# The expert weights of a mixture-of-experts encoder layer: four-chunk transfers for experts 4 to 27, and two chunks of expert 3 read ahead of the down projection of expert 2

## What is computed

```
logits = ht.astype(jnp.float32) @ router_w.astype(jnp.float32) + router_b.astype(jnp.float32)
top_vals, top_idx = lax.top_k(logits, TOP_K)
weights = jax.nn.softmax(top_vals, axis=-1)
...
for e in range(N_EXPERTS):
    gu = ht @ w_gate_up[e] + b_gate_up[e]
    gate, up = gu[:, :D_FF], gu[:, D_FF:]
    gate = jnp.minimum(gate, SWIGLU_LIMIT)
    up = jnp.clip(up, -SWIGLU_LIMIT, SWIGLU_LIMIT)
    act = gate * jax.nn.sigmoid(SWIGLU_ALPHA * gate) * (up + 1.0)
    out = out + combine[:, e:e + 1] * (act @ w_down[e] + b_down[e])
```

## Time and profile before

| | |
|---|---|
| median of three runs | 1233.26 us |
| the profiled execution, its own time | 1233.55 us |
| its span in the trace | 1231.6 us |
| TensorE busy | 97% of the span |
| DMA engines busy from 320 us to 1200 us | 100% |
| VectorE, ScalarE busy | 36%, 22% |
| expert loads of 4 MiB, of 2 MiB | 53, 64 |

### The profile page before, as it was taken

The page is one execution under the profiler, slowest core; times in us unless marked ns, Lnnn a source line. Parts: engine busy times, 40 slices in busy tenths (PEclk is TensorE's granted clock), DMA queues, the critical chain, the costliest instruction groups (busy, mean ns, idle before and its releaser), DMA issues.

```text
span 1231.6 us, 13787 instructions
## 1 busy us (share of the span) xinstructions
PE 1189.2 (97%) x5866; PEld 641.0 (52%) x5866; DVE 437.9 (36%) x745; ACT 269.4 (22%) x440; POOL 0.2 (0%) x4
## 2 busy tenths in 40 slices
PE   9999999999999999999999999998999999889987
PEld 7899968888533443354444334433533444334332
DVE  7777878755422221212322222211222213112112
ACT  5876546344210000000100000000100101000002
POOL 0000000000000000000000000000000000000000
PEclk9999999999999999989999999999999999999999
DMA  9454425698999999999999999999999999999996
GB/s 317 154 163 146 150 90 172 217 399 340 363 424 428 428 427 427 429 436 429 426 435 429 428 434 432 428 433 434 425 432 432 429 428 433 431 425 426 428 425 253
DMA packets 59660, 455.26 MB, mean 370 GB/s; under 512 B 6122, under 2 KB 22923, under 8 KB 39118
## 3 DMA queue, kind: packets, MB, share of 16 engines
q1 hardware_dynamic: 58022, 454.06, 89.6%
q10 hardware_dynamic: 1576, 0.30, 0.1%
HBM read 453.29 MB, written 1.05 MB: 369 GB/s over the span
## 4 chain that ended last, share of the span: by engine, by line
PE 79%; DMA 16%; DVE 3%; issue 1%; ACT 1%; DVEq 0%; ACTq 0%
PE bank L1245 27%; PE bank L1263 15%; DMA ring<-in_w_gate_up 13%; PE total L935 6%; PE bank L935 5%; PE bank L993 4%; PE total L923 4%; PE bank L923 4%; DMA ring<-in_w_down 3%; PE bank L1231 2%; PE bank L1012 1%; PE total L1277 1%; PE bank L1252 1%; PE total L1245 1%; DVE qk_area L2187 1%
## 5 line engine op out<-in xcount | busy, mean ns | idle before, releaser
L1245 PE MATMUL bank<-ring,hy_area 128*64 128x512 f32 x1984 | 439.7, 596 | 14.6 <-DMA ring<-in_w_gate_up 14.6
L1245 PEld LDWEIGHTS bank<-ring,hy_area 128*64 128x64 f32 x1984 | 145.4, 137 | 289.7 <-issue 259.8
L1263 PE MATMUL bank<-ring,xn_area 128*64 128x512 f32 x992 | 223.3, 602 | 2.4 <-DMA ring<-in_w_down 2.4
L1263 PEld LDWEIGHTS bank<-ring,xn_area 128*64 128x64 f32 x992 | 74.0, 138 | 135.0 <-issue 124.9
L2184 DVE TENSOR_SCALAR qk_area<-bank 128x512 f32<-128x512 f32 x31 | 21.4, 692 | 328.2 <-PE bank L1245 328.2
L1728 ACT ACTIVATE qk_area<-qk_area 128x512 f32<-128x512 f32 x32 | 20.2, 630 | 428.3 <-DVE qk_area L2184 428.3
L2199 DVE SCALAR_TENSOR_TENSOR xn_area_r<-bank,tmp_area,xn_area_r 128x512 fp32r<-128x512 f32 x31 | 23.3, 751 | 206.1 <-ACT xn_area_r L1746 206.1
L1883 DVE TENSOR_TENSOR front_r<-ring,slot_r 128x1024 fp32r<-128x1024 f32 x60 | 73.0, 1222 | 19.5 <-ACT slot_r L1539 19.4
L1746 ACT ACTIVATE xn_area_r<-bank,tmp_area 128x512 fp32r<-128x512 f32 x31 | 21.3, 687 | 239.5 <-PE bank L1263 225.7
L1539 ACT CAST slot_r<-ring 128x1024 fp32r<-128x1024 f32 x60 | 62.8, 1050 | 43.6 <-PE bank L935 23.2
L1012 PE MATMUL bank<-tmp_area_r 128*128 128x512 f32 x124 | 40.5, 448 | 12.7 <-issue 8.6
(11 more groups left out here) (403 smaller groups left out, 1282.4 us busy)
## 6 DMA issues: line engine op xcount, KB each, us to landing
ring<-in_w_gate_up SPq DMA_DIRECT2D x33, 4096.0 KB, 29.1
ring<-in_w_gate_up SPq DMA_DIRECT2D x50, 2048.0 KB, 24.7
ring<-in_w_down SPq DMA_DIRECT2D x20, 4096.0 KB, 31.9
ring<-in_w_in SPq DMA_DIRECT2D x31, 1024.0 KB, 5.6
ring<-in_w_down SPq DMA_DIRECT2D x14, 2048.0 KB, 18.5
ring<-in_w_gate_up SPq DMA_DIRECT2D x22, 1024.0 KB, 9.3
ring<-in_w_down SPq DMA_DIRECT2D x19, 1024.0 KB, 9.8
ring<-in_w_branch_gla SPq DMA_DIRECT2D x4, 1024.0 KB, 5.1
```

The source lines that it names most:

```text
L1245: last = pe.matmul(to[bk][half * CAP:(half + 1) * CAP, :], xeT[:, j, q, :], where(j, c), start=False, stop=(j == GU_CH - 1), skip_group_ch ...
L1263: last = pe.matmul(banks[to][half * CAP:(half + 1) * CAP, :], half_of(turned, f), where(j, c * D + half * 512), start=(f == 0), stop=(f == ...
```

## The change

Three tables of numbers are changed. `AHEAD` gets an entry for expert 2: gate-up chunks 0 and 1 of expert 3 stand ahead of the down chunks of expert 2, in the loads and in the use. The one range `WIDE` becomes two: down transfers of four chunks (eight rows) for experts 4 to 29 (`BY_EIGHTS`), and gate-up transfers of four chunks (four rows) for the groups 1 to 6, experts 4 to 27 (`BY_FOURS`). Before, both held for experts 8 to 27.

```diff
-AHEAD = {0: (4, 6), 1: (0, 2)}
+AHEAD = {0: (4, 6), 1: (0, 2), 2: (0, 2)}
...
-WIDE = (8, E - QUAD)
-
-
-def wide(e):
-
-    return WIDE[0] <= e < WIDE[1]
+BY_EIGHTS = (4, E - 2)
+BY_FOURS = (1, E // QUAD - 1)
+
+
+def by_eights(e):
+
+    return BY_EIGHTS[0] <= e < BY_EIGHTS[1]
...
 def by_fours(g):
 
-    return WIDE[0] <= QUAD * g < WIDE[1]
+    return BY_FOURS[0] <= g < BY_FOURS[1]
...
-        if wide(e) and j % 4 == 0 and slot_of(n) + 4 <= SLOTS:
+        if (by_fours(e // QUAD) if j < GU_CH else by_eights(e)) and j % 4 == 0 and slot_of(n) + 4 <= SLOTS:
             width = 4
...
-                             rows_of(e, j, width, 4 if by_fours(e // QUAD) else 2, 8 if wide(e) else 4)).then_inc(moe_loaded[s], 16)
+                             rows_of(e, j, width, 4 if by_fours(e // QUAD) else 2, 8 if by_eights(e) else 4)).then_inc(moe_loaded[s], 16)
...
-                if wide(e):
-                    pe.wait_ge(actT_rest, e - WIDE[0] + 1)
+                if by_eights(e):
+                    pe.wait_ge(actT_rest, e - BY_EIGHTS[0] + 1)
...
-                elif wide(e):
+                elif by_eights(e):
                     copy_by_eights(e + 1)
```

More of the change, by code:

```diff
@@ L2179, in take_weights, with swiglu @@
                 nc.vector.tensor_copy(cslot[:, columns], source).then_inc(cslot_ready, 1)
-            def swiglu(used, count, made=banks[0:2], by_eights=False):
+            def swiglu(used, count, made=banks[0:2], reorder=False):
                 dve.wait_ge(chunks_used, used)
@@ L2189, in swiglu @@
                 dve.wait_ge(sigm_ready, count)
-                if by_eights:
+                if reorder:
                     u, g = (m.rearrange("p (m b c) -> p m b c", b=2, c=4) for m in (up, sig))
@@ L2228, in _ @@
                 g, q = e // QUAD, e % QUAD
-                swiglu(PLACE[e, GU_CH - 1] + 1, e + 1, gu_banks(e), wide(e))
+                swiglu(PLACE[e, GU_CH - 1] + 1, e + 1, gu_banks(e), by_eights(e))
                 if q == QUAD - 1 and g < GROUPS - 1:
```

## The result

The changed kernel takes **1236.59 us** (median of 8 runs, 1236.38 to 1238.80), the kernel before 1233.14 us beside it (8 runs). The ratio is 1.0034, with a 95% interval of 1.0024 to 1.0043: slower by 3.4 us by the medians, 3.0 to 5.3 by the interval. The profiled execution took 1236.38 us, its span is 1234.6 us.

What follows compares the result with a forecast made beforehand. The stream of expert weights through saturated DMA engines was taken as the bound. Terms of -0.7, 0, 3.3 and 0.9 us summed to +3.5 on the profiled 1233.55, giving a median of 1236.7 us, range 1232.5 to 1239.0.

Steps and rivals of the forecast that it cites:

- What bounds the kernel: Saturated DMA engines streaming expert weights set the end; PE work is free unless a load's lead falls under 2.6 us.
- Term A: Wider transfers: 52 chunks of experts 4 to 7, 28 and 29 go from two to four per transfer; -0.7 us.
- Term B: Two chunks of expert 3 ahead of expert 2's down: expert 4's first load has 4.2 us lead; cost 0.
- Term C: Expert 3's longer stall from the gather by four delays expert 5's first load; the stream stands for 3.3 us.
- F: Issue time of expert 5's first load: 428.0 with a short clock drop, 426.8 with clock kept, 430.0 with long drop.
- rival 1: The clock is kept in expert 3, the stream stands 2.1 us there; sum +2.3, 1235.6 us; 20% chance.
- short drop: Main forecast: lowered clock at expert 3's gather, as in expert 11, stall of 14.9 us; 1236.7 us, 37%.
- The signs: DMA share under 1 at 427 to 431 us, gather weight loads twice as long, granted clock under 1.00 there.
- rival 2: Expert 3's gather has the long clock drop, as in expert 7; sum +5.5, 1238.8 us; 22% chance.
- long drop: Lowered clock at expert 3's gather as in expert 7, stall of 16.9 us; the stream stands for 5.3 us.
- Term D: Expert 6's first load awaits down chunk 9 of expert 4; lead 1.7 us, the stream stands another 0.9 us.
- Rival 3: The queue never runs dry, with expert 3's stall at most 11.6 us; only the wider transfers' gain remains: 1232.6 us; 15%.

Runs made afterwards that it cites:

- e5: The kernel before with 2.0 us more TensorE work (repeated transposes) in expert 3; 1233.20 us, ratio 0.9997.
- d4: The kernel before with one wait moved, so the second pair of expert 5 is issued four chunks later, planned lead 0.5 us; 1236.85 us.
- d5: The kernel before with one wait moved, so the second pair of expert 5 is issued five chunks later, planned lead -2.5 us; 1240.12 us.
- e1: The changed kernel with gate-up of experts 4 to 7 back at two rows and two chunks per transfer, gather by two; 1233.16 us.
- e9: The changed kernel with gather by two for experts 4 to 7 and four-chunk gate-up transfers (two 16 KiB pieces) only from expert 6's chunk 4; 1232.87 us.
- e7: The changed kernel without the two chunks of expert 3 ahead of expert 2's down chunks; 1236.92 us.
- e2: The changed kernel with gather by four kept, but gate-up of experts 4 to 7 loaded two chunks at a time; 1235.02 us.
- e8: The changed kernel with the first gate-up transfers of experts 5 and 6 split into pairs; 1235.40 us.
- e4: The changed kernel with expert 3's four transposes done four times over, 2.0 us more planned on TensorE; 1237.77 us.
- e3: The changed kernel with only the first transfer of expert 5 (chunks 0 to 3) split into two pairs; 1236.65 us.
- e6: The changed kernel with gather by two; four-chunk gate-up transfers for experts 4 to 7 bring two pairs of rows each; 1235.29 us.

## Why the prediction was right, and where it was not

**What bounds the kernel** held: e5 adds PE time without effect, d4 and d5 take away lead alone and cost all of it.

**Term A** (-0.7 us) is too small to be seen in the medians: e1 with 24 of the 52 chunks and e9 with more are 0.2 and 0.1 us faster, within their intervals. In the changed kernel's trace it stands as 0.4 to 0.5 us given back behind 462 us. The rates of the earlier trace rows, 428 and 430 GB/s, were printed too coarsely for it.

**Term B** was put at nothing, because a lead of 4.2 us exceeded 2.6. PE's side held: the gate-up of expert 3 ends 0.1 us earlier (0.25 forecast). But the stream still has a hole of 0.9 us by the packets at the first load of expert 4, whose lead was 3.9. Without the two chunks ahead (e7) the hole there is 2.6 us, and that difference is worth only 0.3 us of the total.

**Term C** named the right load and the right place. F was put at 426.8 with the clock kept, and the profiled execution shows 426.77, granted clock 1.00. So in that execution the branch of rival 1 was taken (forecast 1235.6), not the short drop, and the median of 1236.59 is 1.0 us above that branch. The size that failed was the needed lead, "the other 2.6 us are a start that a queued transfer hides". The row behind it, holds both a start (1.0 us to the first packet) and the end of a load up to its landing, and the prediction let the stream run at full rate until the landing before. It didn't: the hole is 2.6 us by the packets and 3.1 by the window, where 2.1 were forecast for this branch. The earlier trace rows had a sign of it. The window 310 to 320, read by its bytes, misses 10 x 143 / 422 = 3.4 us, at a lead of about nothing.

**The sum** met the median partly by luck. Forecast were -0.7, 0, 3.3 and 0.9 us for the terms A to D, 3.5 in all. The changed kernel's packets have -0.5, 0.9, 2.6 and 0.7, 3.7 in all, and 3.4 were measured. A clock drop that was counted on, and that the profiled execution doesn't have, made up for a hole that was put at nothing and for a needed lead that was too short.

**The signs.** The DMA share falls where it was to fall, and the first load of expert 5 landed 12.1 us behind its issue (12.3 forecast). The weight loads in the gather take 330 ns in place of 195, not twice as long, and the granted clock in the profiled execution is 1.00, not less.

**The clock drop** is nevertheless real. The profiled executions of e2 and e7 show it at the gather of expert 3; windows of e2, then e7:

```profile
413.00:425.00 12.00, 10.98 (x46) 8.14 (x44) 3.87 (x7) 2.05 (x4) 0.00 (x0) 0.86 1.01 434
```

```profile
413.00:425.00 12.00, 10.98 (x42) 8.36 (x40) 3.55 (x6) 2.06 (x4) 0.00 (x0) 0.71 1.01 437
```

Those two executions took 1236.30 and 1240.18 us, 1.3 and 3.3 over their kernels' medians. Five of the changed kernel's eight runs lie between 1236.38 and 1236.62, the others at 1237.68, 1238.31 and 1238.80, the top of them where rival 2 put the long drop (1238.8). None of these three was profiled, so that the drop made them is argued, not shown. The experiments with gather by two at this place have no run more than 1.3 us above their median, the kernel before none more than 1.8; e2, e7 and e8, with gather by four, have some at 3.1 to 3.4 above. e4, also by four, has one at 1.8, and e3 has none.

**Term D** (0.9 us at expert 6) stands in the window 456 to 462 with 1.0. It was forecast with a lead of 1.7 and a start of 2.6; the profile has a lead of 2.8, and the longer lead that is needed makes up for it. Twelve chunks from F on landed 459.6 - 426.8 = 32.8 us later, not 31.9.

**Rival 3**, a queue that never runs dry, is refuted by the window at 424. Its bound, F below 424.7, was itself too lax, as e6 shows.

## What to carry to other kernels

Where the DMA engines are saturated, follow the lead of each load, not the busy engines: landing of the transfer ahead minus issue. A wider transfer waits for more slots at once and spends lead; give it only to loads that have more of it than the stream needs, measured in the running stream by moving one wait. Check a rate over a short window against the DMA share beside it before you build on it. And judge a schedule by its tightest load: holes don't add, so mending one that is not the last moves it and changes nothing.

## What was not expected of the hardware

A running stream wanted 3 to 5 us of lead where a single transfer's time to landing suggested 2.6. Of that only 1.0 us lies between the issue and the first packet; the DMA engines ran dry up to 3.4 us ahead of the landing that the trace notes. The Trainium skill ("DMA: Bandwidth & Descriptors", Anatomy of one DMA — SWDGE (gpsimd) path) gives about 2.0 us of fixed cost for one DMA, fitted for DMAs that GpSimd issues. Here SyncE issues them, and the trace has 2.6 for a weight chunk into an empty queue (5.1 us less 2.5 of data).

Pieces of 32 KiB per partition ran at 431.2 GB/s where pieces of 16 KiB ran at 428.4, in one stretch of one execution each, with e1, e3, e4, e6 and e9 in line with it.
